# Normalising by token block, loading six weight tiles beside the ring, and filler products on TensorE

## The chip, the cores and the metric

The kernel runs on one core of a Trainium2 chip. The time is that of one execution on the device, in microseconds; the lower the better. The program is one launch: all weights come from the chip's memory in 1 MB tiles, and nothing but the result goes back.

## The reference

One sequence of 256 tokens with 1024 features, in float32, runs through two stacks of two layers.

- First stack, per layer: `h = rms_norm(x)`, one wide product `h @ w_in`, three kinds of attention, a gated merge `g0*(ya@w_pa) + g1*(yb@w_pb) + g2*(yc@w_pc)`, then `x = x + merged @ w_out`. After it `h = rms_norm(x)`, `u = conv(h @ w_up)`, `x = x + (silu(gate_u) * val_u) @ w_down`.
- Second stack, per layer: a product `x @ w_in`, an RWKV-7 recurrence, a gated convolution with a layer norm, a short convolution, the same kind of gated merge and output product, then `x = layernorm(alpha*x + mix)`. In layer 0 a dense SwiGLU follows, in layer 1 a mixture of 8 experts with the top 2 per token; both end in `x = layernorm(alpha*x + f)`.

```
x = x + merged @ w_out[i]
h = rms_norm(x, mlp_norm[i])
u = causal_depthwise_conv(h @ w_up[i], conv_w[i], conv_b[i])
x = x + (jax.nn.silu(gate_u) * val_u) @ w_down[i]
...
x = _layernorm(alpha * x + mix, ln1_g[i], ln1_b[i])
x = _layernorm(alpha * x + f, ln2_g[i], ln2_b[i])
```

## The kernel before

The residual `xr` holds 256 tokens as two token blocks (TB = 2) of 128 rows, 1024 columns each. A product that follows needs the features on the partitions, so at each change of stage ("transition") the normalised rows are transposed by TensorE: eight feature tiles k for each of the two blocks, 16 transpositions (`turn_wide`, L536). There are eight of them: tags b1 and f1 in both layers of the first stack, b2 and f2 in both layers of the second. ScalarE then copies each transposed tile from its bank, rounded, to `x_hi` (`x_hi_out`, L1081), and VectorE writes the remainder to `x_lo` (`x_lo_out`, L1451). The product is done as three products of rounded parts (`features_split`, L566): hi by hi, lo by hi, hi by lo.

Weights come as 1 MB units of 2048 columns in one order, the stream. SyncE issues all their loads in that order into a ring of four slots (L480); unit u goes to slot u % 4, once unit u - 4 has been used. One layer of the first stack has 21 input units, 4 projection units, 4 output units and 33 units of the feed-forward part; one mixer of the second stack has 24 + 4 + 4. `project` (L600) waits until all four projection units have landed and then does twelve branches; it counts each of the four as used only after the last branch. `project_out` (L622) waits for the last merged branch and then adds four units of row products in banks 0 to 3 (`rows`, L555): bank 2*tb + half for token block tb. The feed-forward part ends in such rows too (`rows_split`, L588).

After the last row product of a stage VectorE adds the banks to `xr` for both blocks. In an RMS transition ScalarE sums squares of block 0, then block 1; VectorE makes the mean of both in one instruction, GpSimd raises it to -1/2 (L2129), VectorE scales both blocks (`rms_apply`, L1484). In a layer-norm transition (`layer_norm`, L1680) ScalarE first sums the rows of both blocks (L1244), VectorE makes the negative means, ScalarE sums the squares (L1249) while VectorE multiplies by the gain (L1686), GpSimd makes the power for both, VectorE scales and adds the bias (L1694).

Before the experts, TensorE computes router logits (L955), VectorE ranks them, TensorE counts places (L961 to L965), VectorE writes a selection, and TensorE gathers the first expert's tokens (L971). VectorE then subtracts the rounded part (L2014) and after that fills table columns for up to three more turns with many small instructions (L2026 to L2041); its splits of expert weights (L2072) come behind these in its queue. The experts' turns follow in a loop. At the end the last expert's rows go through `y_m` (half by ScalarE, half by VectorE), are scattered by TensorE (L980), added by VectorE, normalised, and stored by one transfer (L528).

Every engine works through its own instructions in program order. All waits are on counters, written out by hand with names (`V.of("x_lo", ...)`, `T.of("unit", u)`).

Of the kernel before, what the change touches and what calls it, by code (L numbers as in the profile page):

```python
# [8 lines left out]
F32 = mybir.dt.float32  # L9
# [90 lines left out]

MOE_SLOT = Rotation(MOE_RING, MOE_RING_LATE, MOE_TURNOVER)
# [94 lines left out]
def emit(nc, known, stream, par_d, cst_d, rows_d, x_d, out_d, n_stages):  # L196

    ctx = ExitStack()
    with ctx:
# [77 lines left out]
        s_x = ctx.enter_context(nc.semaphore("x_loaded"))  # L277
# [3 lines left out]
        s_slot = [ctx.enter_context(nc.semaphore(f"slot{i}_loaded")) for i in range(RING)]  # L281
        s_moe_slot = [ctx.enter_context(nc.semaphore(f"moe_slot{i}_loaded")) for i in range(MOE_RING)]
        block = ctx.enter_context(nc.Block())

        def slot(u):
            return ring[:, (u % RING) * UNIT:(u % RING + 1) * UNIT]

        def slot_lo(u):
            return ring_lo[:, (u % RING) * UNIT:(u % RING + 1) * UNIT]

        def loaded(u):
            return s_slot[u % RING], 16 * (u // RING + 1)

        def moe_slot(i):
            b = MOE_SLOT.at[i]
            return slot(b) if b < RING else (yT, xT)[b - RING]
# [5 lines left out]
        def moe_part(w, i):  # L302
            b = MOE_PART.at[i]
            if b < SPLIT:
                return w[:, b * UNIT:(b + 1) * UNIT]
            return w_hi_3 if w is w_hi else w_lo_3

# [134 lines left out]
        lnx = Z[:, 17536:19584].rearrange("p (b n) -> p b n", b=TB)  # L442
# [25 lines left out]
        def _(sp):  # L468
            sp.dma_start(xr, x_d.rearrange("(b p) n -> p b n", p=P)).then_inc(s_x, 16)

            heads = [(par, par_d, PAR.at["attn_norm0"][1], s_par), (cst, cst_d, CST.at["ident"][1], s_const)]
            for to, src, w, _ in heads:
                sp.dma_start(to[:, 0:w], src[:, 0:w]).then_inc(s_head, 16)
            n_main = {1: LAYER1, 2: 2 * LAYER1, 3: FFN_0 + FFN, 4: MOE_0}[n_stages]
            ffn_starts = [l * LAYER1 + N_IN1 + N_PROJ + N_OUT for l in range(DEPTH)] + [FFN_0]
            for u in range(n_main):
                if u >= RING:
                    split = any(f <= u - RING < f + FFN for f in ffn_starts)
                    sp.wait_ge(*(V.of("lo", u - RING) if split else T.of("unit", u - RING)))
                sp.dma_start(slot(u), stream[u]).then_inc(s_slot[u % RING], 16)  # L480
                if u == 1:
                    for to, src, w, sem in heads:
                        sp.dma_start(to[:, w:], src[:, w:]).then_inc(sem, 16)
            if n_stages == 4:
# [3 lines left out]
                def first_free(i):  # L488

                    b = MOE_SLOT.at[i]  # L490
                    if b < RING:
                        return T.of("unit", max(u for u in range(MOE_0) if u % RING == b))
# [32 lines left out]
            sp.wait_ge(*V.of("final"))  # L525
            if n_stages >= 3:
                sp.wait_ge(*G.of("final"))
            sp.dma_start(out_d.rearrange("(b p) n -> p b n", p=P), xr).then_inc(s_out, 16)  # L528
            sp.wait_ge(s_out, 16)
# [3 lines left out]
        def _(pe):  # L533
            mm = nc.tensor.matmul

            def turn_wide(src, tag, l, ready):  # L536

                for k in range(KT):
                    for tb in range(TB):
                        if k == 0:  # L540
                            pe.wait_ge(*ready[tb])
                        t = nc.tensor.transpose(banks[k // 2][:, (k % 2) * SEQ + tb * P:(k % 2) * SEQ + (tb + 1) * P],
                                                src[:, tb, k * P:(k + 1) * P], ct("ident"))
                    t.then_inc(*T.done("turned", tag, l, k))
# [10 lines left out]
            def rows(src, w, first, last):  # L555

                wv = w.rearrange("p (c n) -> p c n", c=2)
                for c in range(2):
                    for tb in range(TB):
                        for half in range(2):  # L560
                            r = mm(banks[2 * tb + half], src(c)[:, tb * P:(tb + 1) * P],  # L561
                                   wv[:, c, half * 512:(half + 1) * 512], start=(first and c == 0),
                                   stop=(last and c == 1))
                return r

            def features_split(bank, w, x, halves=(0, 1)):  # L566

                for c in halves:
                    for k in range(KT):
                        at = slice(k * 256 + c * P, k * 256 + (c + 1) * P)  # L570
# [17 lines left out]
            def rows_split(j, n):  # L588

                for c in range(2):  # L590
                    for tb in range(TB):
                        for half in range(2):
                            for a, b in ((h_hi, w_hi), (h_lo, w_hi), (h_hi, w_lo)):
                                r = mm(banks[2 * tb + half], a[:, j % 2, c, tb * P:(tb + 1) * P],  # L594
                                       part(b, n)[:, c * D + half * 512:c * D + (half + 1) * 512],
                                       start=(j == 0 and c == 0 and a is h_hi and b is w_hi),
                                       stop=(j == FJ - 1 and c == 1 and b is w_lo))
                return r

            def project(l, blk, splits, u0, last_ready):  # L600

                for n in range(N_PROJ):
                    pe.wait_ge(*loaded(u0 + n))
                k_at = [0, splits[0], splits[0] + splits[1]]
                late = BRANCHES[blk][-1][1]
                for n, (c, b) in enumerate(BRANCHES[blk]):
# [5 lines left out]
                    for half in range(2):  # L612
                        for k in range(k_at[b], k_at[b] + splits[b]):
                            wv = slot(u0 + k // 2).rearrange("p (c n) -> p c n", c=2)
# [4 lines left out]
                for n in range(N_PROJ):  # L619
                    T.steps[("unit", u0 + n)] = T.steps[("branch", blk, l, 11)]  # L620

            def project_out(l, blk, u0):  # L622
                for n in range(N_OUT):
                    u = u0 + n
                    pe.wait_ge(*loaded(u))
                    pe.wait_ge(*V.of("merged", blk, l, 11))
                    at = 8 * BRANCHES[blk][0][1] + 2 * n
                    rows(lambda c: gk[:, at + c, :], slot(u), n == 0, n == N_OUT - 1).then_inc(*T.done("unit", u))

            def block1(l):  # L630
# [3 lines left out]
                turn_wide(wide, "b1", l, [V.of("normed", "b1", l, tb) for tb in range(TB)])  # L634

                def half(n, c):
                    u = u0 + n
                    if c == 0:
                        pe.wait_ge(*V.of("lo", u))
                        if n == 0:  # L640
                            pe.wait_ge(*V.of("x_lo", "b1", l))
# [3 lines left out]
                    r = product(banks[4 + n % 2], (in_half(n), slot_lo(u)), (x1_hi, x1_lo), (c,))  # L645
# [61 lines left out]
                turn_wide(wide, "f1", l, [V.of("normed", "f1", l, tb) for tb in range(TB)])  # L707
                f0 = u0 + N_IN1 + N_PROJ + N_OUT
                for (kind, j), n in FFN_UNIT.items():
                    u = f0 + n  # L710
                    pe.wait_ge(*V.of("lo", u))
                    if n == 0:
                        pe.wait_ge(*V.of("x_lo", "f1", l))
                    if kind == "down":
                        pe.wait_ge(*V.of("hidden1", l, j))
                        r = rows_split(j, n)
                    else:
                        if j >= 2:
                            pe.wait_ge(*V.of("conv", kind, l, j - 2))
                        r = features_split(banks[4 + 2 * (j % 2) + (kind == "up")], *ffn_parts(n))  # L720
                    r.then_inc(*T.done("unit", u))
                    T.same((kind, l, j), ("unit", u))

# [8 lines left out]
            def swiglu():  # L732

                for (kind, j), n in FFN_UNIT.items():
                    u = FFN_0 + n
                    pe.wait_ge(*V.of("lo", u))
                    if n == 0:
                        pe.wait_ge(*V.of("x_lo", "f2", 0))
                    if kind == "down":
                        pe.wait_ge(*V.of("dense_hidden", j))  # L740
                        r = rows_split(j, n)
                    else:
                        if j >= 2:
                            pe.wait_ge(*V.of("dense_hidden", j - 2))
                        r = features_split(banks[4 + 2 * (j % 2) + (kind == "up")], *ffn_parts(n))
                    r.then_inc(*T.done("unit", u))
                    T.same(("dense_" + kind, j), ("unit", u))

# [136 lines left out]
            def mixer(l, u0):  # L885
                ready = [V.of("final_x", DEPTH - 1) if l == 0 else V.of("x2", 0, tb) for tb in range(TB)]
                turn_wide(xr, "b2", l, ready)
# [10 lines left out]
                for n in range(7):  # L898
                    pe.wait_ge(*V.of("lo", u0 + n))
                    if n == 0:  # L900
                        pe.wait_ge(*V.of("x_lo", "b2", l))
# [1477 lines left out]
```

## Time and profile before

| | us |
|---|---|
| median of three runs | 2882.07 |
| lowest, highest | 2877.96, 2884.68 |
| the profiled execution's own time | 2881.7 |
| its span, first to last instruction | 2879.9 |

The mean granted clock of TensorE is 0.962 of full speed. Over the span TensorE is busy 93%, VectorE 63%, ScalarE 44%, GpSimd 5%. "Idle before" names how long an engine stood still before an instruction, and the arrow what released it. One float32 product of 512 columns shows as two records of TensorE.

### The profile page before, as it was taken

What the parts mean: (1) busy time and instruction counts of PE and PEld (TensorE: products, weight loads), DVE (VectorE), ACT (ScalarE), POOL (GpSimd) and SP (SyncE); (2) the same over time, 40 slices, a digit from 0 to 9 for tenths busy, and PEclk for the clock granted to TensorE, in tenths of its full rate; (3) what the DMA queues carried; (4) which work ended last, traced back from release to release, by engine and by line L of the source; (5) the groups of instructions that cost most, each with busy time, mean ns of one, the idle gap of its engine ahead of it and who ended that gap; (6) DMA issues with size and microseconds to landing.
All of it is one profiled execution on the core that took longest, in us unless ns stands there. A gap on an engine that the chain in (4) does not pass through costs nothing.

```text
span 2879.9 us, 39065 instructions
## 1 busy us (share of the span) xinstructions
PE 2672.2 (93%) x15410; PEld 2278.7 (79%) x15410; DVE 1821.1 (63%) x2206; ACT 1261.5 (44%) x1440; POOL 145.7 (5%) x117
## 2 busy tenths in 40 slices
PE   7998998998899999988997999878999999999997
PEld 7875997886798888866997888747888888888885
DVE  5643775853676336534554355328888888888887
ACT  4441544451444321103334211116766766766665
POOL 1100000200000011200000023000000000000000
PEclk9998998999999999999998999979999999999998
DMA  6324443323454321125553211146988989898895
GB/s 245 109 103 156 176 181 117 132 103 122 171 193 159 128 92 45 59 91 192 180 189 118 102 59 45 44 190 263 362 338 340 360 335 343 343 363 335 340 346 187
DMA packets 76995, 558.31 MB, mean 194 GB/s; under 512 B 8640, under 2 KB 8768, under 8 KB 9536
## 3 DMA queue, kind: packets, MB, share of 16 engines
q1 hardware_dynamic: 76000, 551.19, 51.4%
q0 software_dynamic: 864, 5.24, 0.5%
q8 instruction: 97, 1.59, 0.2%
q14 instruction: 34, 0.28, 0.0%
HBM read 555.36 MB, written 1.05 MB: 193 GB/s over the span
## 4 chain that ended last, share of the span: by engine, by line
PE 54%; issue 33%; DVE 8%; ACT 2%; DMA 2%; POOL 1%; DVEq 0%; SPq 0%; POOLq 0%; ACTq 0%
PE bank L572 23%; PE bank L594 6%; PE bank L551 6%; PE bank L561 4%; PE bank L616 4%; DMA ring<-in_stream 2%; DVE yT L1788 1%; PE bank L581 1%; PE bank L822 1%; PE bank L833 1%; DVE x_lo L1455 1%; PE bank L692 1%; PE bank L676 1%; PE bank L675 0%; PE bank L684 0%
## 5 line engine op out<-in xcount | busy, mean ns | idle before, releaser
L2072 DVE TENSOR_TENSOR w_lo<-ring,w_hi 128x2048 fp32r<-128x2048 f32 x216 | 486.0, 2288 | 48.2 <-ACT w_hi L1402 48.1
L1402 ACT ACTIVATE w_hi<-ring 128x2048 fp32r<-128x2048 f32 x216 | 404.0, 1917 | 18.6 <-PE bank L996 16.7
L1464 DVE TENSOR_TENSOR w_lo<-ring,w_hi 128x2048 fp32r<-128x2048 f32 x99 | 226.8, 2291 | 161.0 <-ACT w_hi L1093 158.7
L996 PE MATMUL bank<-w_hi,xe_hi 128*128 128x512 f32 x792 | 312.3, 394 | 11.3 <-DVE w_lo L2072 9.3
L996 PE MATMUL bank<-w_lo,xe_hi 128*128 128x512 f32 x792 | 309.7, 391 | 0.0
L996 PE MATMUL bank<-w_hi,xe_lo 128*128 128x512 f32 x792 | 309.3, 390 | 0.0
L572 PE MATMUL bank<-x_hi,w_hi 128*128 128x256 f32 x1056 | 300.6, 285 | 5.5 <-DVE x_lo L1455 5.5
L1093 ACT ACTIVATE w_hi<-ring 128x2048 fp32r<-128x2048 f32 x99 | 189.3, 1912 | 260.6 <-DMA ring<-in_stream 155.3
L572 PE MATMUL bank<-x_lo,w_hi 128*128 128x256 f32 x1056 | 300.2, 284 | 0.0
L572 PE MATMUL bank<-x_hi,w_lo 128*128 128x256 f32 x1056 | 300.2, 284 | 0.0
L551 PE MATMUL bank<-xT,ring 128*128 128x256 f32 x1088 | 248.7, 387 | 1.1 <-ACT Z L1329 1.1
L572 PE MATMUL bank<-x_hi,ring_lo 128*128 128x256 f32 x832 | 238.3, 286 | 0.0
L551 PEld LDWEIGHTS bank<-xT,ring 128*128 128x128 f32 x1088 | 208.4, 194 | 34.0 <-issue 3.2
L572 PEld LDWEIGHTS bank<-x_hi,w_hi 128*128 128x128 f32 x1056 | 204.2, 193 | 7.7 <-DVE x_lo L1455 6.6
L572 PEld LDWEIGHTS bank<-x_lo,w_hi 128*128 128x128 f32 x1056 | 204.2, 193 | 1.1
L572 PEld LDWEIGHTS bank<-x_hi,w_lo 128*128 128x128 f32 x1056 | 204.0, 193 | 0.0
L572 PE MATMUL bank<-x_hi,in_hi 128*128 128x256 f32 x608 | 182.2, 300 | 8.8 <-DVE x_lo L1455 5.4
L996 PEld LDWEIGHTS bank<-w_hi,xe_hi 128*128 128x128 f32 x792 | 149.3, 189 | 44.7 <-DVE w_lo L2072 12.1
L996 PEld LDWEIGHTS bank<-w_lo,xe_hi 128*128 128x128 f32 x792 | 149.2, 188 | 31.7
L572 PE MATMUL bank<-x_lo,in_hi 128*128 128x256 f32 x608 | 173.8, 286 | 0.0
L996 PEld LDWEIGHTS bank<-w_hi,xe_lo 128*128 128x128 f32 x792 | 149.3, 189 | 30.4
L1022 PE MATMUL bank<-w_hi,hT_hi 128*128 128x512 f32 x396 | 163.5, 413 | 0.0
(342 smaller groups left out, 5176.5 us busy)
## 6 DMA issues: line engine op xcount, KB each, us to landing
ring<-in_stream SPq DMA_DIRECT2D x439, 1024.0 KB, 4.9
yT<-in_stream SPq DMA_DIRECT2D x54, 1024.0 KB, 6.5
xT<-in_stream SPq DMA_DIRECT2D x27, 1024.0 KB, 7.0
norm_rows<-in_rows POOLq DMA_DIRECT2D x4, 1024.0 KB, 6.0
cst<-in_cst SPq DMA_DIRECT2D x1, 2145.0 KB, 19.9
par<-in_par SPq DMA_DIRECT2D x1, 1502.0 KB, 15.3
xres<-in_x SPq DMA_DIRECT2D x1, 1024.0 KB, 5.2
group_rows<-in_rows POOLq DMA_DIRECT2D x2, 512.0 KB, 8.0
```

Source lines behind the costliest of these rows:

```text
L551: r = mm(bank[:, c * SEQ:(c + 1) * SEQ], wv[:, k, c * P:(c + 1) * P], xk[:, k, :], start=(k == 0), stop=(k == KT - 1))
L561: r = mm(banks[2 * tb + half], src(c)[:, tb * P:(tb + 1) * P], wv[:, c, half * 512:(half + 1) * 512], start=(first and c == 0), stop=(last ...
L572: r = mm(bank[:, c * SEQ:(c + 1) * SEQ], w[a][:, at], x[b][:, k, :], start=(k == 0 and a == b), stop=(k == KT - 1 and a == 1))
L581: r = mm(bank[:, tb * SEQ:(tb + 1) * SEQ], x[b][:, k, tb * P:(tb + 1) * P], w[a][:, k * 256:(k + 1) * 256], start=(k == 0 and a == b), sto ...
L594: r = mm(banks[2 * tb + half], a[:, j % 2, c, tb * P:(tb + 1) * P], part(b, n)[:, c * D + half * 512:c * D + (half + 1) * 512], start=(j = ...
L616: r = mm(bank[:, half * SEQ:(half + 1) * SEQ], wv[:, k % 2, col:col + P], yk[:, k, :], start=(k == k_at[b]), stop=(k == k_at[b] + splits[b ...
L996: r = mm(banks[4 + j % 2], a[:, k, :], moe_part(b, i)[:, q * 512:(q + 1) * 512], start=(k == 0 and a is xe_hi and b is w_hi), stop=(k == K ...
L1022: r = mm(banks[half], a[:, j % 2, c * P:(c + 1) * P], moe_part(b, i)[:, c * D + half * 512:c * D + (half + 1) * 512], start=(j == 0 and c ...
L1093: act_(part(w_hi, n), slot(f0 + n), ACT.Copy).then_inc(*A.done("hi", f0 + n))
L1402: act_(moe_part(w_hi, at), moe_slot(at), ACT.Copy).then_inc(*A.done("moe_hi", at))
L1464: v.tensor_tensor(part(w_lo, n), slot(f0 + n), part(w_hi, n).bitcast(F32), ALU.subtract)\
L2072: v.tensor_tensor(moe_part(w_lo, at), moe_slot(at), moe_part(w_hi, at).bitcast(F32), ALU.subtract)\
```

## The change

- Homes. Two of a layer's units no longer go to the ring: in the first stack the first two projection units, in the second stack the first two output units. They go to two places in the scratch area Z that are free by then. The other units take the four ring slots in turn.
- `project` waits for each unit where a branch first needs it, and a unit counts as used after the last branch that reads it. In the second stack the stream now brings the convolutions' two projection units ahead of RWKV's two. `project_out` waits, for each unit, for the merged branches of that unit's rows alone.
- The last unit of row products does block 0 first. VectorE, ScalarE and GpSimd normalise by token block; `turn_wide` transposes block 0, then fillers, then block 1, into banks 0, 1, 6, 7. Fillers are products of the identity with 512 columns of constants in bank 4, whose result nothing reads.
- The first product after a transition waits for `x_lo` tile by tile. In layer norms the addition gives the row sums too, which ScalarE's pass gave before.
- Router: fillers ahead of three waits, the gather in two halves, the table columns in few wide instructions and ahead of the subtraction. At the end ScalarE copies both halves of `y_m`, and the residual is combined before the scatter lands. The input and the result are moved in two transfers each.

```diff
+def homes():
+    aside = {}
+    for l in range(DEPTH):
+        for n in range(2):
+            aside[l * LAYER1 + N_IN1 + n] = RING + n
+            aside[(MIX2_0, MIX2_1)[l] + N_IN2 + N_PROJ + n] = RING + n
+    out = []
+    for u in range(MOE_0):
+        out.append(aside.get(u, sum(v not in aside for v in range(u)) % RING))
+    return out
...
-                if u >= RING:
-                    split = any(f <= u - RING < f + FFN for f in ffn_starts)
-                    sp.wait_ge(*(V.of("lo", u - RING) if split else T.of("unit", u - RING)))
-                sp.dma_start(slot(u), stream[u]).then_inc(s_slot[u % RING], 16)
+                if HOME[u] in HOME[:u]:
+                    user = max(w for w in range(u) if HOME[w] == HOME[u])
+                    split = any(f <= user < f + FFN for f in ffn_starts)
+                    sp.wait_ge(*(V.of("lo", user) if split else T.of("unit", user)))
+                if HOME[u] >= RING:
+                    l = u // LAYER1 if u < MIX2_0 else int(u >= MIX2_1)
+                    sp.wait_ge(*(T.of("sumsq", l, len(QK_PAIRS) - 1) if u < MIX2_0 else T.of("o", l, 3)))
+                sp.dma_start(slot(u), stream[u]).then_inc(s_slot[HOME[u]], 16)
...
+            def keep_busy(n):
+                for _ in range(n):
+                    mm(banks[4], ct("ident"), cst[:, 0:512], start=True, stop=True)
+
+            def turn_wide(src, tag, l, ready, between, behind=1):
+                for tb in range(TB):
+                    if tb:
+                        keep_busy(between)
+                    pe.wait_ge(*ready[tb])
+                    for k in range(KT):
+                        at = (k % 2) * SEQ + tb * P
+                        t = nc.tensor.transpose(turn_bank(k)[:, at:at + P], src[:, tb, k * P:(k + 1) * P], ct("ident"))
+                        if tb:
+                            t.then_inc(*T.done("turned", tag, l, k))
+                keep_busy(behind)
...
-                for n in range(N_PROJ):
-                    pe.wait_ge(*loaded(u0 + n))
+                unit_of = [(0, 1, 2, 3), (2, 3, 0, 1)][blk == "b2"]
...
+                            if u not in here:
+                                pe.wait_ge(*loaded(u))
+                                here.add(u)
...
-                    pe.wait_ge(*V.of("merged", blk, l, 11))
+                    pe.wait_ge(*V.of("merged", blk, l, max(i for i, (c, b) in enumerate(BRANCHES[blk]) if c == n)))
...
+            def rms_norm(tag, l, source):
+                if source:
+                    residual(*source, 0)
+                rms_mean(tag, l, 0)
+                if source:
+                    residual(*source, 1)
+                rms_apply(tag, l, 0)
+                rms_mean(tag, l, 1)
+                rms_apply(tag, l, 1)
...
+                centre(0)
+                variance(0)
+                centre(1)
+                scale(0)
+                variance(1)
+                scale(1)
...
+                keep_busy(3)
                 pe.wait_ge(*V.of("selected"))
...
+                keep_busy(1)
                 pe.wait_ge(*V.of("pick0"))
-                gather().then_inc(*T.done("gather0"))
+                gather("gather0")
+                keep_busy(2)
```

In the new `layer_norm`, `centre(tb)` adds the block's two bank halves with row sums, makes its negative mean and applies the gain; `variance(tb)` follows ScalarE's sum of squares; `scale(tb)` follows GpSimd's power. `between` and `behind` are 4 and 1 at f1 and at b1 of layer 1, 0 and 0 at b1 of layer 0, 1 and 1 at b2 of layer 0, and 5 and 1 at b2 of layer 1 and at both f2.

## Rows read from the trace of the kernel before

**Rows 1.** The waits, TensorE's; us in total, times, longest.
```profile
PE bank L542 <- DVE Z L1490: 31.6, 7, 10.9
PE bank L542 <- DVE xres L1694: 29.2, 6, 9.1
PE bank L561 <- DMA ring<-in_stream: 19.4, 4, 4.9
...
PE bank L616 <- DMA ring<-in_stream: 15.4, 4, 4.9
PE bank L996 <- DVE w_lo L2072: 9.3, 1, 9.3
```

**Rows 2.** The chain that ended last, 196 to 245 us; start, us, what.
```profile
198.81 4.81 DMA ring<-in_stream
...
233.10 4.87 DMA ring<-in_stream
```

**Rows 3.** The timeline around the second stack's projection; start, us, engine, line.
```profile
1244.96 1.09 ACT L1344 ACTIVATE yT<-yT,par 128x256 f32<-128x256 f32 x2
1247.94 8.74 PE L616 MATMUL bank<-yT,ring 128*128 128x256 f32 x32 [4.93 <-DMA ring<-in_stream]
```

**Rows 4.** Stretches; length, busy us by engine, then PEclk, DMA share, GB/s.
```profile
203.80:206.80 3.00, 3.00 (x8) 2.44 (x9) 2.56 (x3) 0.00 (x0) 0.00 (x0) 0.52 0.00 0
238.00:244.30 6.30, 6.29 (x8) 2.68 (x9) 0.00 (x0) 0.00 (x0) 0.00 (x0) 0.50 1.02 430
281.60:285.20 3.60, 3.60 (x17) 3.60 (x18) 2.29 (x1) 0.74 (x1) 0.00 (x0) 0.50 0.02 5
744.00:747.40 3.40, 3.40 (x28) 3.40 (x29) 2.29 (x1) 0.72 (x1) 0.00 (x0) 1.00 0.00 0
933.80:937.20 3.40, 3.29 (x16) 2.88 (x14) 3.18 (x4) 2.86 (x8) 0.00 (x0) 0.51 0.00 0
937.30:940.50 3.20, 0.57 (x5) 0.60 (x6) 3.20 (x11) 1.16 (x5) 0.00 (x0) 1.00 0.00 0
1923.80:1930.00 6.20, 6.19 (x30) 6.09 (x29) 4.45 (x2) 3.00 (x2) 0.00 (x0) 0.50 0.20 82
1975.00:2855.00 880.00, 880.00 (x4050) 716.38 (x4048) 763.28 (x583) 610.71 (x519) 0.00 (x0) 1.00 0.90 342
```

**Rows 5.** The timeline of the RMS transition at f1, layer 0.
```profile
261.79 7.03 PE L561 MATMUL bank<-ring,gates 128*128 128x512 f32 x16
...
268.86 2.48 DVE L1499 SCALAR_TENSOR_TENSOR xres<-bank,xres 128x512 f32<-128x512 f32 x4 [4.69 <-PE bank L561]
...
274.74 1.42 DVE L1490 TENSOR_SCALAR Z<-xres,small 128x1024 f32<-128x1024 f32 x2 [0.82 <-POOL small L2129]
...
276.21 3.46 PE L542 MATMUL bank<-cst,Z 128*128 128x128 f32 x15 [0.19 <-DVE Z L1490]
```

**Rows 6.** The timeline of the layer-norm transition at f2, layer 0.
```profile
1314.37 2.48 DVE L1931 SCALAR_TENSOR_TENSOR xres<-xres,bank 128x512 f32<-128x512 f32 x4 [4.61 <-PE bank L561]
...
1321.98 2.48 DVE L1694 SCALAR_TENSOR_TENSOR xres<-Z,small,norm_rows 128x1024 f32<-128x1024 f32 x2 [0.81 <-POOL small L2129]
```

**Rows 7.** The timeline from the router to the first expert.
```profile
1923.02 6.97 PE L955 MATMUL bank<-par,xT 128*128 128x8 f32 x32 [0.94 <-DVE xT L1449]
...
1936.45 5.83 PE L971 MATMUL bank<-gates,xres 128*128 128x128 f32 x32 [0.98 <-DVE gates L2005]
...
1957.01 2.29 DVE L2072 TENSOR_TENSOR w_lo<-ring,w_hi 128x2048 fp32r<-128x2048 f32 x1
```

**Rows 8.** The timeline of the last gather and of the tail.
```profile
2845.70 3.73 PE L971 MATMUL bank<-gates,xres 128*128 128x128 f32 x32
...
2857.81 1.94 PE L980 MATMUL bank<-gates 128*128 128x512 f32 x3 [2.68 <-DVE gates L2104]
...
2874.67 0.40 SPq L528 DMA_DIRECT2D out<-xres  x1
```

**Rows 9.** The timeline of the start.
```profile
16.93 3.22 DVE L1455 SCALAR_TENSOR_TENSOR x_lo<-bank,par,x_hi 128x256 fp32r<-128x256 f32 x8
```

More of the change, by code:

```diff
@@ L618, in project @@
                     r.then_inc(*T.done("branch", blk, l, n))
-                for n in range(N_PROJ):
-                    T.steps[("unit", u0 + n)] = T.steps[("branch", blk, l, 11)]
+                    for k in range(k_at[b], k_at[b] + splits[b]):
+                        T.same(("unit", u0 + unit_of[k // 2]), ("branch", blk, l, n))
             def project_out(l, blk, u0):
@@ L1925, in mixer @@
                         ffn_split(FFN_0, n)
-                ve.wait_ge(*T.of("unit", u0 + MIX2 - 1))
-                for tb in range(TB):
-                    for half in range(2):
-                        d = xr[:, tb, half * 512:(half + 1) * 512]
-                        v.scalar_tensor_tensor(out=d, in0=d, scalar=ALPHA, in1=banks[2 * tb + half], op0=ALU.mult,
-                                               op1=ALU.add).then_inc(*V.done("mix", l, tb))
-                own()
-                layer_norm("ln1", l, "x1")
+                layer_norm("ln1", l, "x1", lambda tb: T.of("rows", "b2", l, tb), add_rows)
                 (x_lo_out if l == 0 else xT_out)("f2", l, None)
@@ L2044, in _ @@
-                V.same(("turns",), ("column",))
+                own()
+                v.tensor_tensor(which, mine, grow(ct("slots", 0, 8), [P, MORE, 8], 1), ALU.mult).then_inc(*V.done("which"))
+                for q in range(MORE):
+                    v.tensor_tensor(theirs[:, q, :, :], grow(mine[:, q, :], [P, 6, 8], 1), every[:, :, 0:8], ALU.mult)\
+                        .then_inc(*V.done("theirs"))
+                own()
+                v.tensor_reduce(sm("whom", MORE), which, AX.X, ALU.add).then_inc(*V.done("whom"))
@@ new lines, in _ @@
+                for q in range(MORE):
+                    v.tensor_reduce(every[:, :, 8 + q:9 + q].rearrange("p t c -> p (t c)"), theirs[:, q, :, :], AX.X, ALU.add)\
+                        .then_inc(*V.done("column"))
+                own()
+                v.tensor_copy(turn_cells[:, 1:1 + MORE], sm("whom", MORE)[0:1, :]).then_inc(*V.done("cells"))
+                v.tensor_scalar(place[:, :, 8:8 + MORE], place[:, :, 8:8 + MORE], -float(P), None, ALU.add)\
+                    .then_inc(*V.done("cells"))
@@ L2102, in _ @@
                 V.leave()
[L2103 to L2110 removed]
+                ve.wait_ge(*T.before("gather", 1))
                 for tb in range(TB):
```

342 lines of the change are left out of this document (166 added, 176 removed).

## The prediction

> **What bounds the kernel.** I read three views in this order. First the busy time by stretch: in the experts' stretch TensorE is busy for 880 of 880 us at full clock [rows 4], so nothing that the change does there can show; what can be won lies before 1975 us and after the last turn. Then TensorE's own waits: the largest are for normalised rows, 31.6 and 29.2 us over the transitions, then 19.4 and 15.4 us for weights, four waits of each kind, then one of 9.3 us for a split of expert weights [rows 1]. The chain of waits shows that the weight waits are on the path: 4.81 and 4.87 us behind a load that is issued when the unit before it is released [rows 2]. Last the granted clock: after each such stop it is 0.50 to 0.52, the lower of the two levels (1.2 against 2.4 GHz), for some microseconds of real work [rows 4]. A stop is therefore paid twice: its length, and half of the low stretch behind it.
>
> Below, t = 0 is the end of the last row product of a stage, and "worth" counts both payments.
>
> **Part 1, the homes.** All four projection units can be in before the projection starts, and two of the output units before it ends; the fourth output unit loads from the last branch on (4.87 us [rows 2]) and isn't needed until 3 units of 6.9 us each have run (16 records take 7.03 us with the last one's tail, 0.43 each [rows 5]). The stream's later units wait for the same output units as before.
> - Output, four times: the stop goes whole, 19.4 us together [rows 1]. The merged branches aren't late: only the last unit's chunk is merged after the projection. The low stretch behind is 6.3 us in the first layer [rows 4], and 3.2, 4.3 and 4.0 us in the other three (same view): half of 17.8 is 8.9.
> - Projection, first stack, twice: four products of the third attention's norm stand inside the gap, so TensorE starts 2.8 us earlier, not 4.8. 5.6 us, and half of the 3.0 [rows 4] and 3.2 low: 3.1.
> - Projection, second stack, twice: here another wait is late next. The projection also waits for the convolution branch, whose activation ends at 1246.05 where the weights let it go at 1247.94 [rows 3]. 1.9 of 4.93 us goes, twice 1.85 = 3.7, and a stop of 3 us stays. The clock may still fall in it: of half of 6.4 low I count a third, 1.1.
> Sum 19.4 + 8.9 + 5.6 + 3.1 + 3.7 + 1.1 = 41.8. Ends: 34 if the low stretches stay at 0.5 as they are in half of the eight places, 46 if the last 3 us stop costs no clock. SyncE issues in order, and the new loads' extra condition (the last sum of squares; RWKV's last output) stands ahead of later loads; both conditions are met well before those loads' own slots come free, so nothing queues behind them.
>
> **Part 2, RMS transitions** (f1 twice, b1 of layer 1). Before: four additions 2.48 us, two sums of squares, the mean and power, the scaling 1.42 us, 16 transpositions until 279.67, splitting; the first product comes at 281.60, 12.7 us after t = 0 at 268.83 [rows 4, 5]. After, by block: block 0's rows end at -3.4 (half of the last unit). Its two additions take 1.25, ScalarE's pass with its read 1.25, the mean and power 1.0: ready at -0.1. But VectorE's queue has block 1's additions (0 to 1.3) ahead of block 0's scaling: rows of block 0 at 2.0. Block 1: sum to 2.6, power to 3.5, scaling to 4.2. TensorE: eight transpositions. At the low clock they take 0.22 each (15 in 3.46 [rows 5]); the trace has none at the high one, but products of the same 128 columns run at 0.117 there against 0.182 (32 in 3.73 [rows 8], 32 in 5.83 [rows 7]). I take 0.9 us for eight, as the gap of 2 us is shorter than those that cost clock; ends 0.9 and 1.8. Transposed by 2.9; four fillers follow. A filler isn't in the trace; the nearest row is an output product of 512 columns in float32, 0.86 us at the high clock [rows 5] and 1.7 at the low (8 records in 6.3 us [rows 4]). So the fillers run to 6.3, though block 1 is ready at 4.2: **they overshoot by 2.1 us**. Transpositions to 7.2, one filler to 8.05; two copies by ScalarE and one remainder (0.42 each) make the first x_lo at about 8.25. The product starts at 8.3 and runs at the 0.42 us of VectorE per tile instead of 0.36, 0.5 more: 8.8. Gain 3.9 per f1; at b1, where 14.2 us passed before, 5.4. Low stretches: 3.6 [rows 4] at the first f1 and 5.7 at b1 (same view), none at the second f1, as its row at 744 shows [rows 4]: 1.8 + 2.85. Sum 3.9 + 3.9 + 5.4 + 4.65 = 17.9; ends 5 (below) and 26 (fillers that hide).
>
> **Part 3, layer norms** (f2 of layer 0, b2 of layer 1). Before, 15.3 and 16.3 us from t = 0 to the product, and 3.6 us low after both: 17.1 and 18.1. After: block 0's additions with sums, mean, gain (1.24) lie before t = 0; block 1's additions, mean and gain run to 2.9; then block 0's scaling (1.24 each; two are 2.48 [rows 6]) to 4.2, and block 1's variance, power, scaling to 6.4. The sum that the addition now gives is not in the trace; from 0 to 0.19 us each (a read of ScalarE's sum), I take 0.05. TensorE stands still for 4.2 us, and such a stop costs the clock. Five fillers, 4.3 us at the high and 8.5 at the low clock, start at 6.0 in the low one and see it rise: end at 11.7 +- 0.7, five after block 1's readiness. Transpositions and splitting: product at 13.5. Gains 3.6 and 4.4 (there memory clears and a weight split of VectorE, 3.3 us, fit beside the fillers). 8.0; ends -2 and 15.
>
> b2 of layer 0 has no norm: before 9.0 us and 3.5 low. Block 0's rows are ready at once, block 1's at 1.3; then VectorE's clears and split end at 5.0, and x_lo follows: product at 5.5, plus half the chance of a low clock, 0.9. Gain 4.2. Start: tile-wise waiting lets the product begin 2.8 us before the end of x_lo's 3.22 us [rows 9]; the next unit's split, behind a constants load, leaves 1.7.
>
> A rule is weighed here. The 16 transpositions of b2 stand in 933.8 to 937.2 at 0.51, and the clock is 1.00 right behind, though no product had come [rows 4]. The Trainium skill ("TensorE: Matmul & The Clock Gate", Part 4: PE-mode transpose) says that full clock does not engage for transposes, as they don't count as busy in the same way. The trace disagrees. By the rule the fillers alone would hold the clock, and at the RMS transitions 2.9 us would pass uncounted before them: that is rival B.
>
> **Part 4, the router.** Before: t = 0 at 1908.4; logits 1923.0 to 1930.0, 7.0 us [rows 7]; ranking 3.1; places 2.3; selection 1.0; gather 5.83; 2.1 to the first expert product at 1944.36; it then stops for 9.3 us [rows 1] because VectorE's table columns (some 70 small instructions until 1957) stand ahead of the split [rows 7]. The second near unit starts at 1959.35, then 5.3 us low (same view as rows 4), 2.65: 53.6. After: norm and fillers bring the logits to 13.4 (14.6 before). They ran wholly low for 6.2 us [rows 4] although busy, so I keep 5.5 of 7.0. Ranking takes 3.1; three fillers beside it last 2.6 or 5.1, I take 3.8. Places 1.9, selection 1.0, gather 4.3 (3.73 to 5.83), two fillers 1.9; the columns, now 16 instructions of 0.15 to 0.2, about 3.2 us, hide behind the gather. Then 24 products of 0.227: 5.5. Sum 13.4 + 5.5 + 3.8 + 1.9 + 1.0 + 4.3 + 1.9 + 5.5 = 37.3, so 16.3; with a share of low clock left, 15. Ends 7 (all low) and 22 (all high).
>
> **Part 5, the tail.** Before, the scatter starts at 2857.81, since VectorE copies half of y behind its splits [rows 8]; ScalarE alone is ready at 2856.4. Residuals (2.36) end at 2859.5, beside the scatter. By block, with the durations of part 3: last scaling ends at 2869.1; the store went out at 2874.67 [rows 8]. 5.6, and half the bytes behind it: 6.2 (5 to 7).
>
> **Sum.** 41.8 + 17.9 + 8.0 + 4.2 + 1.7 + 15 + 6.2 = 94.8. From the profiled execution's 2881.7 (span 2879.9, 0.4 below the median shown): **2787**. 41 fillers are in it, at 35 us if all run high.
>
> **Rivals.**
> - C, the waits go altogether: the clock never falls, fillers hide in real waits, since the rows come later than I reckon but start earlier work. 46 + 24 + 12 + 5 + 2 + 22 + 7 = 118, less 6 for RWKV's own phases: 2770. For it: a row of full clock at the second f1 [rows 4]. Against: the 4.2 us stop of each layer norm.
> - B, fillers at the low clock: each 1.7 us; a transition then ends at 14.9 (RMS) or 18.3 (layer norm), no better than before. Parts 2 to 5 give 15 in place of 53: 2881.7 - 42 - 15 = 2825. For it: the low logits [rows 4].
> - E, the homes don't take: weights still come 4.9 us late, since SyncE stands before one of the new conditions. 2881.7 - 53 = 2829. Against it: the conditions' places in the order.
> - D, slower: in the transitions the fillers stand on the path whole, at the low clock, and the blocks' order gives nothing because block 0's scaling waits behind block 1's additions. 41 x 1.7 = 70 us more, less 42 and 6: 2904. It decides once the fillers' cost passes what parts 1 and 5 give, 48. For it: in every transition I already find more filler than wait. Against: block 0 is nearly done before t = 0.
>
> **Numbers.** Forecast 0.62, C 0.15, B 0.13, E 0.07, D 0.03. The forecast's own range is 2774 to 2803; taking in C's most part and B's near half, 2766 to 2826. A run set of this kernel can tell 0.2%, 6 us, from no change: faster 0.96, within 0.01, slower 0.03.
>
> **What would show it.** TensorE's waits for ring loads at the projection and output lines gone, but about 3 us twice at the second stack's projection. Product starts 8.3 us (RMS) and 13.5 us (layer norm) after t = 0, with the fillers ending 2 and 5 us after block 1's last scaling; were they to end before it, my chain is too short. No wait for an expert split near 1950. The last scaling some 14 us after the last expert product instead of 19.5. Wrong would be: a low clock through the RMS transitions, or TensorE waiting behind a new load.

## The result and the profile after

| | median, us | lowest to highest | ratio to before, 95% |
|---|---|---|---|
| before | 2880.25 | 2877.96 to 2884.68 | |
| changed | 2784.66 | 2779.0 to 2787.09 | 0.9664 [0.9644, 0.9683] |
| forecast | 2787 | 2766 to 2826 | |

The change makes the kernel 3.4% faster; the median is 2.3 us from the forecast. The profiled execution took 2785.75 us, its span 2783.9 against 2879.9; TensorE's mean granted clock is 0.982 (0.962 before).

TensorE's waits of the changed kernel (the groups that answer to [rows 1]; us in total, times, longest):

```profile
PE bank L577 <- DVE Z L1534: 19.4, 5, 11.4
PE bank L577 <- DVE small L1753: 12.7, 3, 4.4
PE bank L663 <- ACT yT L1386: 6.2, 2, 3.1
PE bank L1030 <- ACT gates L1473: 1.2, 1, 1.2
```

No wait for a ring load is left, none for an expert split, and at the projection of the second stack (L663) the forecast stop of 3.1 us stands twice, behind ScalarE's activation. The chain of waits, where [rows 2] showed two loads (start, us, what), now has projection and output products end to end, at a granted clock of 1.00:

```profile
199.77 27.63 PE bank L663 x128
227.39 27.48 PE bank L597 x64
```

The RMS transition at f1 of layer 0 (timeline; answers to [rows 5]). Row products end at 254.87, which is t = 0:

```profile
256.90 1.09 PE L577 MATMUL bank<-cst,Z 128*128 128x128 f32 x8 [2.04 <-DVE Z L1534]
257.83 3.60 PE L567 MATMUL bank<-cst 128*128 128x512 f32 x8
258.28 0.76 DVE L1534 TENSOR_SCALAR Z<-xres,small 128x1024 f32<-128x1024 f32 x1 [0.66 <-POOL small L2189]
261.27 1.04 PE L577 MATMUL bank<-cst,Z 128*128 128x128 f32 x8
263.25 0.36 PE L612 MATMUL bank<-x_hi,w_hi 128*128 128x256 f32 x1
```

Block 1 is scaled at 259.04, and four fillers (8 records, L567) hold its transpositions until 261.27: 2.2 us past need (2.1 forecast), product at 8.4 (8.3). The layer norm at f2 of layer 0, t = 0 at 1260.92 (answers to [rows 6]):

```profile
1265.07 1.09 PE L577 MATMUL bank<-cst,xres 128*128 128x128 f32 x8 [4.16 <-DVE small L1753]
1265.75 1.28 DVE L1759 SCALAR_TENSOR_TENSOR xres<-Z,small,norm_rows 128x1024 f32<-128x1024 f32 x1 [0.67 <-POOL small L2189]
1266.00 6.15 PE L567 MATMUL bank<-cst 128*128 128x512 f32 x10
1271.99 1.04 PE L577 MATMUL bank<-cst,xres 128*128 128x128 f32 x8
1273.67 0.36 PE L612 MATMUL bank<-x_hi,w_hi 128*128 128x256 f32 x1
```

Here TensorE stands for 4.16 us, the five fillers begin at the low clock (6.15 us; 4.46 where all run high), and block 1, scaled at 1267.03, waits until 1271.99 behind them: 5.0 us past need, as forecast. The router (answers to [rows 7]):

```profile
1852.47 3.71 PE L1001 MATMUL bank<-par,xT 128*128 128x8 f32 x32 [0.31 <-DVE xT L1492]
1856.03 4.52 PE L567 MATMUL bank<-cst 128*128 128x512 f32 x6
1863.51 5.46 PE L1018 MATMUL bank<-gates,xres 128*128 128x128 f32 x32
```

and the tail (answers to [rows 8]; the last expert product ends at 2767.63, the span at 2783.9):

```profile
2768.80 3.70 PE L1030 MATMUL bank<-gates 128*128 128x512 f32 x8 [1.18 <-ACT gates L1473]
2778.74 2.44 SPq L553 DMA_DIRECT2D out<-xres  x2
2779.52 1.28 DVE L1759 SCALAR_TENSOR_TENSOR xres<-Z,small,norm_rows 128x1024 f32<-128x1024 f32 x1 [0.74 <-POOL small L2189]
```

### The profile page after: what moved, and what is told of

It is laid out like the page before. It is cut to its first block, busy times and chain, and to the rows that moved or that the text cites. A ratio compares the mean times of both kernels' runs of the same rounds, so it can differ in the third digit from the quotient of the medians.

```text
span 2783.9 us, 39210 instructions
## 1 busy us (share of the span) xinstructions
PE 2677.4 (96%) x15492; PEld 2273.1 (82%) x15492; DVE 1815.7 (65%) x2178; ACT 1253.0 (45%) x1425; POOL 148.7 (5%) x125
## 4 chain that ended last, share of the span: by engine, by line
PE 56%; issue 34%; DVE 7%; ACT 1%; DMA 1%; POOL 1%; SPq 0%; POOLq 0%; DVEq 0%; ACTq 0%
PE bank L612 23%; PE bank L587 6%; PE bank L635 6%; PE bank L663 4%; PE bank L597 4%; PE bank L567 1%; DVE yT L1864 1%; PE bank L621 1%; DMA cst<-in_cst 1%; PE bank L869 1%; PE bank L880 1%; PE bank L739 1%; PE bank L723 1%; PE bank L722 1%; PE bank L731 0%
## 6 DMA issues: line engine op xcount, KB each, us to landing
par<-in_par SPq DMA_DIRECT2D x1, 1502.0 KB, 17.1
```

## The experiments

Theory M, mine: the parts are worth what the sum gives them, and the fillers stand past need on the path because block 0 comes late in VectorE's queue. Rival F: the fillers are a net gain as they stand, by the clock they hold. Each kernel was timed in five rounds beside the kernel before, whose median was 2888.05, 2881.64 and 2887.88 us on the chips of the three sets; kernels of one set ran on one chip, and kernels of different sets are compared by their ratios to the kernel before. "Product" is the start of the first product behind the transpositions, counted from t = 0, and "60 products later" is the start of the product 60 places behind it.

### The changed kernel again, and the homes alone

The first has no edit and is the measure for its set. The second is the kernel before with the part on weight homes only, what `project` and `project_out` wait for included:

```diff
+HOME = homes()
 ...
-        s_slot = [ctx.enter_context(nc.semaphore(f"slot{i}_loaded")) for i in range(RING)]
+        s_slot = [ctx.enter_context(nc.semaphore(f"slot{i}_loaded")) for i in range(RING + 2)]
 ...
-                if u >= RING:
 ...
+                if HOME[u] in HOME[:u]:
```

> The changed kernel itself, run beside the three others so that they can be read against it on one chip. Both theories: 2785 (2779 to 2791), 0.967 of before. Anything outside would mean that chips differ by more than the effects looked for in the other three.

Measured: 2779.87 (2777.70 to 2787.52), ratio 0.9639 [0.9617, 0.9661].

> The kernel before with the part on weight homes alone (loads, their order and what the projection waits for), nothing of the blocks' order and no fillers. My sum says 41.8 us: 2839 against 2881, ratio 0.985 (2833 to 2846). Rival 1, the parts overlap (a stop removed here only moves its low clock to the next transition): less than 31 us, 2850 or more. Rival 2, the homes carry most of the change: 2825 or less.

Measured: 2837.25 (2835.06 to 2839.65), ratio 0.9836 [0.9816, 0.9855], which is 47 us (42 to 53); between the profiled spans, 2879.9 and 2833.2, it is 46.7. The sum had 41.8 and an upper end of 46. Both rivals fall. The rest of the change was not run alone; as a difference it is 2837 - 2780 = 57 us, against 53 forecast.

### No fillers

```diff
-                for _ in range(n):
+                for _ in range(0):
```

> The changed kernel without any of its filler products (all 41 left out; what is computed stays the same). Theory M (fillers stand past the need, on the path): block 1 is ready 2 us (RMS) and 5 us (layer norm) before its transpositions start, so the three layer norms' products start at about 9 us after t = 0 instead of 13.0 to 14.4, the RMS ones at about 7 instead of 8.4 to 10.1; against it each transition gets a low stretch of some 3.6 us behind it, which costs 1.8. Net 0 at the RMS norms, 2 to 3 us at each layer norm, near nothing at the router, where the fillers stand beside VectorE's ranking: 2777 (2768 to 2785). Theory F (fillers earn their time through the clock): the transpositions and all first products run at 1.2 GHz, some 4 us lost at each of eight places and nothing won: 2790 or more, and granted clock back at the 0.96 of before.

Measured: 2769.19 (2765.57 to 2776.81), ratio 0.9604 [0.9581, 0.9627]: 10.7 us faster than the changed kernel of the same set. Its timeline at the same layer norm, t = 0 at 1256.23:

```profile
1260.39 3.98 PE L577 MATMUL bank<-cst,xres 128*128 128x128 f32 x16 [4.16 <-DVE small L1753]
1264.40 0.55 PE L612 MATMUL bank<-x_hi,w_hi 128*128 128x256 f32 x1
```

The transpositions run at the low clock (3.98 for sixteen, against 1.09 and 1.04 for eight each), yet the product comes at 8.2 instead of 12.8. At the f1 norms it comes at 6.5 and at 7.4 at b1, but a low stretch follows, and of the 1.9 us gained at f1 of layer 0 only 0.8 are left 60 products later (15.06 instead of 15.82 us). M holds and F falls: as placed, the 41 fillers cost more than they save.

### Block 0 scaled first, with and without fillers

```diff
                 rms_mean(tag, l, 0)
+                if tag == "f1":
+                    rms_apply(tag, l, 0)
                 if source:
                     residual(*source, 1)
-                rms_apply(tag, l, 0)
+                if tag != "f1":
+                    rms_apply(tag, l, 0)
 ...
                 variance(0)
+                scale(0)
                 centre(1)
-                scale(0)
                 variance(1)
```

> The changed kernel with block 0 scaled ahead of block 1's additions, at both f1 norms and all layer norms (not at b1 of layer 1, whose scaled rows lie where weights are still read). Fillers unchanged. Theory M: the fillers start when block 0 is transposed, so what block 0 gains, the product gains: about 1.2 us at each f1 and 4 us at each layer norm (block 0 scaled at about 1 us after t = 0 instead of 4.2), and the fillers then just fill the gap (overshoot 0.3 us at f1 and 0.5 at the layer norms). 12 + 2.4 and some clock: 2769 (2762 to 2777). Rival: block 0's sum and power aren't done when its scaling comes up, VectorE stands still before block 1's additions, and block 1 becomes late by as much: 2782 or more.

Measured: 2766.21 (2764.96 to 2770.41), ratio 0.9589 [0.957, 0.9609]: 13.7 us faster than the changed kernel. The same layer norm, t = 0 at 1256.05:

```profile
1257.68 1.09 PE L577 MATMUL bank<-cst,xres 128*128 128x128 f32 x8 [1.63 <-DVE xres L1762]
1258.61 4.46 PE L567 MATMUL bank<-cst 128*128 128x512 f32 x10
1262.90 1.04 PE L577 MATMUL bank<-cst,xres 128*128 128x128 f32 x8
```

The stop is 1.63 us instead of 4.16, all fillers run high, block 1 (scaled at 1262.51) waits 0.4 us, and the product comes at 8.5 instead of 12.8; at f1 it comes at 7.1 instead of 8.4 or 10.1. At b2 of layer 1 it comes only at 11.0 (14.2 in the changed kernel), since VectorE's memory clears and a split of weights now end last there.

The second kernel of this pair has the same order and no filler:

> Block 0 scaled first, and no filler at all. It tells what fillers are worth when they fit the gap. Theory M: with block 0 scaled first the fillers end within 0.5 us of block 1's readiness, so leaving them out wins nothing and costs the clock: block 1's eight transpositions at 1.9 instead of 0.95 us, and a low stretch behind that costs 1.8. 2 to 3 us at two f1 and three layer norms, 3 at the router: 12 us more than the same order with fillers (6 to 18), about 2778 against 2766, ratio 0.963. Rival N (fillers are never worth their time here): 2766 or less, as leaving them out won 10 us in the changed kernel.

Measured: 2779.24 (2777.51 to 2780.42), ratio 0.9646 [0.9631, 0.9661]. Against the same order with fillers it is 16 us slower by the ratios and 13 us by the medians. So a filler is worth something where it fits the gap, and costs where it doesn't: without fillers the changed order gained 10.7 us, this one lost 13 to 16. The product of f2 comes no later (8.5), but it and those behind it run at the low clock: 60 products later it is 16.6 us after t = 0 instead of 15.8, at b2 of layer 1 20.1 instead of 18.3, at f1 of layer 0 16.6 instead of 14.5.

### Fillers ahead of block 0

```diff
-            def turn_wide(src, tag, l, ready, between, behind=1):
+            def turn_wide(src, tag, l, ready, between, behind=1, ahead=0):
+                keep_busy(ahead)
```

> The changed kernel (its order and its fillers unchanged) with more fillers, put ahead of block 0's transpositions, inside the stop that stands there: two in the 2.0 us stops of the RMS transitions, four in the 4.2 us stops of the layer norms. Theory M: that stop is what makes the clock fall, and it is longer than the new fillers (1.8 and 3.6 us), so they cost nothing; the fillers behind then all run at the high clock: layer-norm products at about 11.2 us after t = 0 instead of 12.8 to 14.2, RMS ones at 8.4 always instead of 8.4 or 10.0. 3 x 2 + 0 to 4: 8 us less than the changed kernel, 2775 (2770 to 2780), ratio 0.963, and a smaller spread from run to run. Rival: fillers don't hold the clock where nothing else runs, or more fillers only add: 2785 or more.

Measured: 2773.22 (2766.04 to 2776.58), ratio 0.9607 [0.9585, 0.9629]: 6.7 and 11.4 us below the two medians of the changed kernel. By ratios it is 0.9607 against 0.9639 and 0.9664, and the interval still touches the nearer one's, so the trace has to carry the argument. At f2 of layer 0, t = 0 at 1255.39 (lines are one further down here), four fillers more and an earlier product, at 11.07:

```profile
1259.56 1.09 PE L578 MATMUL bank<-cst,xres 128*128 128x128 f32 x8 [0.73 <-DVE small L1754]
1260.49 4.46 PE L567 MATMUL bank<-cst 128*128 128x512 f32 x10
```

It was the stop ahead of block 0, with nothing in it, that took the clock. Over all traces with unchanged fillers behind it: after stops of 4.2 us with nothing in them the next fillers were low in 9 of 9 cases; after 2.04 us (RMS) in 5 of 12, in the same kernel from one execution to the next; after 2.36 us in 1 of 3; after 1.63 to 1.70 us in 0 of 6; with fillers inside the same 4.2 and 2.04 us stops in 0 of 3 and 0 of 4.

### The convolution's activation earlier

```diff
-                fill(99)
                 sc.wait_ge(*V.of("confn", l))
 ...
                         bias=pr(f"conf_lb{l}", i)).then_inc(*A.done("confy", l))
+                fill(99)
```

`fill(99)` is ScalarE's work for all input units that are left.

> The changed kernel with ScalarE's two convolution activations (and the table load ahead of them) put before the last input units instead of behind them, in both layers of the second stack. My prediction said that a stop of about 3 us stays at this projection because these activations are late, not the weights. Theory M: the wait shrinks from 3.09 to about 0.6 us (the last input unit's own activation) and 5 us go in all: 2775 to 2780, ratio 0.962. Rival: TensorE waits for the weights or for RWKV's gated rows there as well, and the stop stays at 2 us or more: 2782 or more.

Measured: 2782.18 (2771.73 to 2784.74), ratio 0.9649 [0.9628, 0.9671]. The wait at the projection:

```profile
PE bank L663 <- ACT gates L1328: 1.8, 2, 0.9
```

The stop went from 3.1 to 0.9 us in both layers, which shows that the weights had not been what was late. But the total doesn't show it, and the miss is mine: I had counted on the rest standing still. In this profile all three RMS transitions fell to the low clock (products at 10.0 to 10.1 instead of 8.4), and RWKV's phases ahead of the first of the two projections took 2.8 us more than in the faster of the two traces of the unchanged kernel, as much as they vary between those two (309.4 and 312.2 us from t = 0 of b2 to the projection). The gain is 4.4 us in the waits and isn't resolved in the time. Nor is it in the pair of kernels below that differ by this edit alone: 2765.65 without it and 2758.67 with it, ratios 0.9596 and 0.9582, each inside the other's interval.

### VectorE's order, and all together

```diff
                 own()
+                split(0)
+                x_lo_out("b2", l, None)
                 for buf in (xs, us):
                     v.memset(buf, 0.0).then_inc(*V.done("zeroed"))
-                split(0)
-                x_lo_out("b2", l, None)
 ...
-                for i in range(2):
+                def first_split(i):
 ...
+                first_split(0)
 ...
                 one_hot(pick, 0, "sel", "pick0")
+                first_split(1)
```

> Block 0 scaled first as before, fillers as they are, and three things moved on VectorE: two memory clears behind x_lo at both b2 transitions, and the second of the two expert weight splits from ahead of the logits to behind the selection. Theory M: x_lo of b2 starts 1 us earlier in both layers (product at 10.0 instead of 11.0 us after t = 0 in layer 1), and the logits are copied 1.6 us earlier, which moves the gather by the same unless the three fillers (5.5 us from the logits on) end last: 1.0 + 1.0 + 0.5 to 1.6 = 3 us less than with block 0 first alone, 2763 (2760 to 2767). Rival: the fillers behind the logits set the start of the places, and only 2 us go.

Measured: 2765.65 (2760.14 to 2768.21), ratio 0.9596 [0.9578, 0.9614]. The total lies in the expected range, but the 3 us that it was to win over block 0 first alone (2766.21, ratio 0.9589) don't show. b2's product comes at 10.0 instead of 11.0 in layer 1, 4.9 instead of 5.5 in layer 0. In layer 1 that wins nothing: VectorE splits the next unit's weights no earlier than before, TensorE now waits for that split, and 60 products later both kernels stand at 18.27 us. In layer 0 0.9 us are left (13.2 instead of 14.1). The two starts in layer 1, t = 0 at 1447.69:

```profile
1457.67 0.36 PE L612 MATMUL bank<-x_hi,mix_hi 128*128 128x256 f32 x1 [0.50 <-DVE x_lo L1498]
1464.45 0.39 PE L612 MATMUL bank<-x_hi,mix_hi 128*128 128x256 f32 x1 [0.88 <-DVE ring_lo L1789]
```

At the router nothing is won in this trace (first expert product 25.9 us after t = 0, with and without the move), and the rival is right: the places' products still start when the three fillers end (5.47 us at the low clock).

The three edits together:

> Block 0 scaled first, early convolution activations and the three moves on VectorE together: if the parts add up (each sits in a different gap of TensorE), 13.7 + 5 + 3 = 22 us less than the changed kernel: 2758 (2754 to 2763), ratio 0.956. Less than 17 us would mean that a part merely moves another wait into view.

Measured: 2758.67 (2757.97 to 2765.47), ratio 0.9582 [0.9565, 0.96]. The total is the expected one; by the ratios to before it is 16 us under the changed kernel of the first set (21 by the medians). That the parts add up isn't shown, since two of the three didn't show in the time by themselves. In this trace the fillers behind the logits run high (2.82 us), VectorE's ranking ends last, and the first expert product comes at 23.3 us after t = 0 instead of 25.9: there the earlier logits do count, 2.6 us of it together with the clock. How much each of the two gives isn't told apart.

### Fillers in the last stops, and fewer behind the logits

```diff
-                turn_wide(xr, "b2", l, ready, 5 if l else 1)
+                turn_wide(xr, "b2", l, ready, 5 if l else 1, 1, 2 if l else 0)
 ...
-                turn_wide(xr, "f2", l, [V.of("x1", l, tb) for tb in range(TB)], 5)
+                turn_wide(xr, "f2", l, [V.of("x1", l, tb) for tb in range(TB)], 5, 1, 1)
```

> The kernel with all three later moves (block 0 first, early activations, VectorE's order) and fillers ahead of block 0 where a stop of over 1.6 us is left: two at b1 and b2 of layer 1, one at both f2. Theory M: the clock stays up in every transition, which it did in most already: 0 to 3 us less than without them, 2757 (2753 to 2760) and a spread under 4 us. Rival as above: 2760 or more.

Measured: 2756.84 (2755.98 to 2762.09), ratio 0.9551 [0.9533, 0.957]: the lowest median here, 4.5% under before, and below the changed kernel's interval. From the kernel with all three edits (0.9582) it isn't told apart, as the intervals overlap, and the spread of 6 us is over the 4 expected; in its trace the fillers between the blocks run high in all six normed transitions.

The second kernel also has two fillers instead of four between the blocks at b1 of layer 1, and two instead of three behind the logits:

```diff
-                keep_busy(3)
+                keep_busy(2)
```

> The same with the fillers cut where they still stand past need: between the blocks at b1 of layer 1 two instead of four (block 1 ready 4.2 us after t = 0, its transpositions started at 6.9), and behind the logits two instead of three (three take 5.5 us at the low clock beside a ranking of 3.2). Theory M: 1.7 us and 1.8 us less than with all fillers, 2753 (2750 to 2757), ratio 0.956 or below. Rival: the shorter filling lets the clock fall at the gather, 2 us back: no difference.

Measured: 2759.06 (2755.04 to 2765.0), ratio 0.9561 [0.954, 0.9582]: above the 2753 expected and no difference, as the rival said. b1's product came at 7.4 instead of 8.3. At the router the places came 2 us earlier, but at the low clock, and so did the filler and the gather behind them (timeline of this kernel; the row of the gather was 3.84 us without the cut):

```profile
1831.68 3.76 PE L567 MATMUL bank<-cst 128*128 128x512 f32 x4
1839.07 4.63 PE L1019 MATMUL bank<-gates,xres 128*128 128x128 f32 x32
```

The first expert product stands 26.3 us after t = 0 against 25.8 with three fillers.

## Why the prediction was right, step by step

| step | forecast | measured | from |
|---|---|---|---|
| 1, homes | 41.8 | 46.7 | spans, homes alone |
| 2, three RMS transitions | 17.9 | 14.9 | 60 products later, before and changed |
| 3, two layer norms | 8.0 | 7.6 | the same |
| 3, b2 of layer 0 | 4.2 | 3.5 | the same |
| 3, start | 1.7 | 0.5 | t = 0 of f1, changed and homes alone |
| 4, router | 15 | 18.7 | t = 0 to the last expert product |
| 5, tail | 6.2 | 8.4 | last expert product to the end |
| sum | 94.8 | 100.3 | |

The spans differ by 96.0 us in this profile and by 102.7 in the second one of the same kernel, whose span is 2777.2; the sum of the measured parts lies between. That the rest is the scatter of phases that the change doesn't touch is argued, not shown. The mechanisms came as forecast but for the clock behind the 2 us stops and the gain of the start. That the total fell within 2.3 us is in part luck: homes, router and tail gave 4.9, 3.7 and 2.2 us more than forecast, the transitions and the start 5.3 less, and the kernel's own four runs lie 8 us apart. Of the parts of the change only the homes and the fillers were taken apart by runs; the terms of the transitions, router, tail and start are read from traces.

- **Homes.** The mechanism was right: both waits went, the fourth output unit was never waited for, and the stop behind the activation stayed. What was too small is the share of the clock at the second stack's projection, where I took a third of what the low stretch costs, 1.1. With the homes alone the 3 us stop costs no clock in either layer:

```profile
1220.73 7.17 PE L642 MATMUL bank<-yT,ring 128*128 128x256 f32 x32 [3.09 <-ACT yT L1370]
1804.67 7.17 PE L642 MATMUL bank<-yT,ring 128*128 128x256 f32 x32 [3.09 <-ACT yT L1370]
```

  Before, these 32 records took 8.74 and 8.60 us, so 3.0 came back and not 1.1. In the changed kernel they take 7.17 in layer 0 and 8.86 in layer 1, in both of its profiles. Taken stage by stage up to t = 0, the homes give 12.8, 11.1, 10.6 and 10.3, or 44.8; the other 1.9 of the 46.7 lies in stages that they don't touch.
- **RMS.** The product at 8.4 (8.3 forecast) in one of three transitions; in the other two at 10.0 and 10.1. The step that failed is "the gap of 2 us is shorter than those that cost clock": it cost the clock in 5 of 12 cases. With the clock up in all three, as in the second profile of the same kernel, the term is 18.2: 5.8, 8.2 and 4.2. The low stretches that I took from one trace of the kernel before are chance as well: with the homes alone, which leave these transitions as they were, 60 products later is 20.0 us at the first f1 and 21.4 at the second, against 21.6 and 20.0 before.
- **Layer norms.** Stop 4.16 us (4.2), fillers first low and then high, five past need (5.0), products at 12.8 and 14.2 (13.5). The addition with a sum costs 0.08 us more each (0.05).
- **b2 and start.** Product at 5.4 (5.5). At the start it came only 0.8 us earlier, and unit 1 then waits 1.5 us behind the constants load, which I had named and still priced too low. A gain of the start isn't resolved at all: in the eleven profiles of kernels with the changed first stage, t = 0 of the first f1 lies anywhere from 253.6 to 258.0, on both sides of the 255.3 with the homes alone.
- **Router.** First expert product at 30.6 and the second unit, 24 products later, at 36.5 (37.3), at the full clock, with no wait for a split. By the 49th product the gain is 17.1; the other 1.6 of the 18.7 come in the experts' turns, where I had expected nothing. The logits took 3.7 us where I kept 5.5, but the fillers behind them ran low (4.52 for three).
- **Tail.** Last scaling 13.2 us after the last expert product (14, before 19.5). I took 0.6 us for half the store's bytes; from the last scaling to the end it is 3.1 instead of 5.2, 2.1 less. The scatter also runs at the high clock, 3.70 against 5.40 us, behind a stop of 1.2 instead of 2.7 us.
- **Readings and sums.** I wrote that the trace has no transpositions at the high clock. It has: those of RWKV's rows, 1.04 us for eight, which is also what block 1's took later (I used 0.9):

```profile
1256.52 1.04 PE L936 MATMUL bank<-cst,Z 128*128 128x128 f32 x8
```

  The homes' own terms give ends of 35.3 and 43.9, not 34 and 46, the layer norm of b2 gives 4.6, not 4.4, and b2 of layer 0 4.35, not 4.2. None of this moves the forecast by more than 0.4 us.
- **Rivals.** B and E fall with the first profile, D too. C's 46 was nearer for the homes, and its full clock was wrong for the layer norms. Of D a part is true: the fillers stand on the path and cost 10.7 us net. That is a ninth of what the change gives.

The rule that I weighed (the Trainium skill, "TensorE: Matmul & The Clock Gate", Part 4: PE-mode transpose: transpositions don't engage the full clock) can be read once more in the kernel without fillers, where nothing but transpositions stands ahead. At f2, behind sixteen of them without a pause, three products run low (0.55, then 0.41 each) before they shorten towards 0.28; at f1, where eight were separated from eight by 0.68 us, twelve do. At b1 of layer 1 the granted clock is 1.00 in the 1.33 us stop between the sixteenth transposition and the first product. The trace disagrees with the rule again: transpositions brought the clock up before any product had run.

## What to carry to other kernels

A filler is priced twice: by the work that it keeps at the high clock, and by how far it ends past the moment the real operand is ready; put the consumer's first operand ahead in the producer's queue first, then cut the filling to the gap. Fillers belong ahead of the first operand, inside the stop that lets the clock fall, as much as behind it. When a weight load is the last wait at a junction, look for the one right behind it in the same trace (here 3.1 us of ScalarE), and check whether the engine that causes it had been idle before. An earlier first product is worth only what is left of it some products later: at b2 of layer 1 a product that came 1.0 us earlier won nothing.

## What was not expected of the hardware

- The clock after a given stop is not fixed. The 2.04 us stop gave the high clock in seven cases and the low one in five, with the same instructions. The changed kernel's runs go from 2777.7 us (granted clock 0.987) to 2787.5 (0.982), and those of the kernel before in the third set from 2878.6 (0.965) to 2890.1 (0.957): the spread between runs goes with the granted clock.
- Behind products of 8 columns the clock is mostly low: after 32 of them, 3.7 to 5.3 us in which TensorE was busy, the three fillers took 4.5 to 5.5 us in seven of the eight traces that have three, and 2.8 in one, that of the three edits together. Why that one differs stays open: its 32 products took 3.7 us, as in three of the others.
